# A one-core hybrid encoder block: the second half of an expert's down product moves behind the load of the next expert's class

## The reference

```python
def expert_block(args):
    xb, e = args
    return (jax.nn.silu(xb @ w_gate[e]) * (xb @ w_up[e])) @ w_down[e]
...
y = y_pad[dest] * gate_s[:, None].astype(y_pad.dtype)
out = jnp.zeros((T, D), y.dtype).at[tok_s].add(y)
```

## Time and profile before

| | us |
|---|---|
| median of 3 runs | 1718.0 |
| lowest, highest run | 1713.45, 1719.99 |
| the profiled execution: its own time | 1719.35 |
| the profiled execution: span from first to last instruction | 1717.5 |
| PE busy in that span | 1667.0 (97%) |
| DVE, ACT, POOL busy | 746.9, 476.6, 526.0 |

### The profile page before, as it was taken

The page is one execution under the profiler, slowest core; times in us unless marked ns, Lnnn a source line. Parts: engine busy times, 40 slices in busy tenths (PEclk is TensorE's granted clock), DMA queues, the critical chain, the costliest instruction groups (busy, mean ns, idle before and its releaser), DMA issues.

```text
span 1717.5 us, 30945 instructions
## 1 busy us (share of the span) xinstructions
PE 1667.0 (97%) x10740; PEld 1220.9 (71%) x10741; DVE 746.9 (43%) x1756; ACT 476.6 (28%) x1258; POOL 526.0 (31%) x617
## 2 busy tenths in 40 slices
PE   8899999999999999999998899999999999999996
PEld 6667676676756667576657688688778787878784
DVE  1444556544555445555466323332333333333323
ACT  1444333433233342443333111111111111111111
POOL 0101011010110101011012446556565555655553
PEclk9999999999999999999999999999999999999998
DMA  9732233323433234322234879989999999999995
GB/s 345 187 113 69 88 125 116 100 72 98 127 116 92 72 105 128 116 81 79 86 122 151 298 270 366 331 302 344 336 352 360 317 332 326 358 328 355 332 326 168
DMA packets 180051, 360.23 MB, mean 210 GB/s; under 512 B 34806, under 2 KB 65883, under 8 KB 180005
## 3 DMA queue, kind: packets, MB, share of 16 engines
q1 hardware_dynamic: 152980, 304.25, 53.1%
q0 software_dynamic: 26160, 55.26, 9.2%
q10 hardware_dynamic: 864, 0.10, 0.0%
HBM read 311.52 MB, written 76.68 MB: 226 GB/s over the span
## 4 chain that ended last, share of the span: by engine, by line
PE 77%; issue 8%; DMA 5%; DVE 3%; SPq 3%; POOL 2%; ACT 1%; DVEq 0%; ACTq 0%; POOLq 0%
PE bank L366 14%; PE bank L358 13%; PE bank L389 13%; PE bank L1515 10%; PE bank L1502 10%; PE bank L1520 8%; DMA h_dram<-sums_quarters,movec 2%; DMA sums_quarters<-h_dram,movec 2%; PE bank L408 1%; PE bank L521 1%; PE bank L424 1%; SPq L223 1%; POOL xg L1422 1%; PE bank L502 1%; ACT L1566 1%
## 5 line engine op out<-in xcount | busy, mean ns | idle before, releaser
L1502 PEld LDWEIGHTS bank<-xT,wts 128*128 128x128 f32 x2048 | 253.8, 194 | 34.1 <-issue 28.0
L366 PE MATMUL bank<-uT,w_in_sb 128*128 128x128 f32 x2304 | 274.2, 277 | 0.6 <-DMA w_in_sb<-w_in_in 0.6
L366 PEld LDWEIGHTS bank<-uT,w_in_sb 128*128 128x128 f32 x2304 | 263.6, 192 | 12.7 <-issue 10.4
L1502 PE MATMUL bank<-xT,wts 128*128 128x128 f32 (+2 forms) x2048 | 259.2, 287 | 13.8 <-issue 6.0
L358 PE MATMUL bank<-w_in_sb,uT 128*128 128x512 f32 (+1 forms) x768 | 262.3, 494 | 4.9 <-DVE attm L858 2.8
L1515 PE MATMUL bank<-xT,wts 128*128 128x128 f32 (+2 forms) x2048 | 249.8, 283 | 1.9 <-DVE hT L1619 1.9
L1515 PEld LDWEIGHTS bank<-xT,wts 128*128 128x128 f32 x2048 | 246.7, 192 | 2.1 <-DVE hT L1619 2.1
L1034 POOL TENSOR_SCALAR ss<-ss 128x1 f32<-128x1 f32 (+1 forms) x48 | 9.7, 202 | 741.9 <-ACT junk L605 405.5
L1520 PE MATMUL bank<-wts,hT 128*128 128x512 f32 x512 | 232.2, 597 | 0.0
L389 PE MATMUL bank<-w_out_sb,mixT 128*128 128x512 f32 x512 | 223.2, 593 | 0.8 <-ACT mixT L631 0.8
L1422 POOL DMA_INDIRECT xg<-v_dram,idxm x165 | 195.4, 1185 | 67.8 <-issue 32.0
(11 more groups left out here) (263 smaller groups left out, 1737.8 us busy)
## 6 DMA issues: line engine op xcount, KB each, us to landing
wts<-w_gate_in SPq DMA_DIRECT2D x32, 2048.0 KB
wts<-w_up_in SPq DMA_DIRECT2D x32, 2048.0 KB
wts<-w_down_in SPq DMA_DIRECT2D x32, 2048.0 KB
p_dram<-decays_keys_gates SPq DMA_DIRECT2D x60, 192.0 KB, 3.2
pT<-p_dram SPq DMA_DIRECT2D x15, 768.0 KB, 4.3
x_sb<-x_in SPq DMA_DIRECT2D x16, 512.0 KB, 3.5
xT_in<-x_t_in SPq DMA_DIRECT2D x16, 512.0 KB, 4.8
h_sb<-x_in SPq DMA_DIRECT2D x16, 512.0 KB, 5.1
```

The costliest lines, as they stand in the source:

```text
L366: m = pe.matmul(bk[name][0:hi - lo, col:col + P], w_in[:, k, lo:hi], uT[:, k, :], start=k == 0, stop=k == KD - 1)
L1502: m = pe.matmul(G[m_ % 2][:, 0:w], wg[:, k, m_ * P:(m_ + 1) * P], xT[:, k, 0:w], start=k == 0, stop=k == KD - 1)
```

## The change

The second half of the down product leaves `pe_chunk` and becomes `pe_second`, which is one piece of code for all classes. TensorE's loop is rotated: the first half of expert 0 stands ahead of the loop (in all three classes), then for each following expert the class is loaded, the second half of the expert before is done, and then the branch on the class leads to gate, up and first half of this expert. The quarter means' product now stands amid the second half, and for every expert, narrow ones too.

```diff
@@ -1538,12 +1538,15 @@
         pe_down(pe, YB[0], n, 0, main, range(KF - 1, KF)).then_inc(sem("m_d_done"), 2 if w == P else 1)
-        if w > P:
-            after(pe, "m_", "tail_square", n + 1)
-            pe.wait_ge(sem("fw_loaded"), 6 * 16)
-            pe.matmul(U[0][:, 0:2], quad[:, :], part[:, :], start=True, stop=True)
+
+    def pe_second(pe, n):
+
         after(pe, "m_", "summed", 3 * n)
-        pe_down(pe, YB[1], n, 1, main, range(KF)).then_inc(sem("m_d_done"), 1)
+        pe_down(pe, YB[1], n, 1, slice(0, P), range(2))
+        after(pe, "m_", "tail_square", n + 1)
+        pe.wait_ge(sem("fw_loaded"), 6 * 16)
+        pe.matmul(U[0][:, 0:2], quad[:, :], part[:, :], start=True, stop=True)
+        pe_down(pe, YB[1], n, 1, slice(0, P), range(2, KF)).then_inc(sem("m_d_done"), 1)
@@ -1857,8 +1860,12 @@
             pe.wait_ge(sem("meta_ready"), 1)
-            with pe.Fori(0, NE) as e:
-                by_width(pe, chunk_class(pe, e), lambda w: pe_chunk(pe, e, w))
+            by_width(pe, chunk_class(pe, 0), lambda w: pe_chunk(pe, 0, w))
+            with pe.Fori(1, NE) as e:
+                cls = chunk_class(pe, e)
+                pe_second(pe, e - 1)
+                by_width(pe, cls, lambda w: pe_chunk(pe, e, w))
+            pe_second(pe, NE - 1)
```

More of the change, by code:

```diff
@@ L1659, in dve_y_over @@
             .then_inc(sem("o_yD_taken"), 1)
-    return (credit, load, first_base, move, put_sums, scatter_over, gather, gather_over, copy_pieces, copy_index, pe_x_over, pe_chunk, pe_chunk_over, act_silu, act_gate,
+    return (credit, load, first_base, move, put_sums, scatter_over, gather, gather_over, copy_pieces, copy_index, pe_x_over, pe_chunk, pe_second, pe_chunk_over, act_silu, act_gate,
             act_squares, act_rows_over, dve_x, dve_x_over, dve_h, dve_tail, dve_sums, dve_scale, dve_clear, dve_y_over)
@@ L1774, in program @@
         with ExitStack() as mem:
-            (credit, load, first_base, move, put_sums, scatter_over, gather, gather_over, copy_pieces, copy_index, pe_x_over, pe_chunk, pe_chunk_over, act_silu, act_gate,
+            (credit, load, first_base, move, put_sums, scatter_over, gather, gather_over, copy_pieces, copy_index, pe_x_over, pe_chunk, pe_second, pe_chunk_over, act_silu, act_gate,
              act_squares, act_rows_over, dve_x, dve_x_over, dve_h, dve_tail, dve_sums, dve_scale, dve_clear,
```

## The result

| | before | changed |
|---|---|---|
| median of 3 runs, us | 1718.0 | 1748.19 |
| lowest, highest | 1713.45, 1719.99 | 1743.77, 1749.08 |
| ratio, 95% interval | | 1.018 (1.0154 to 1.0207) |
| profiled execution: span, us | 1717.5 | 1741.7 |
| profiled execution: own time, us | 1719.35 | 1743.77 |

The change makes the kernel slower by 1.8%, 30 us of the medians and 24.2 us of the two profiled spans. The point forecast was 1738, the range 1726 to 1749; one of the three executions, at 1749.08, lies just above that range.

A forecast was written before the change was run, and what follows sets the result against it. The expert loop was taken as bound by what PE is given, transfers close behind; wide experts -5.9, narrow experts +18 and code fetches +7.5 us on 1718 gave 1738, range 1726 to 1749.

The forecast's parts named there:

- The three terms: Expert loop: wide experts -5.9 us, narrow experts' new wait +18, code fetches at first visits after the rotation +7.5.
- The signs that the prediction named: Squares' waits of 18 to 25 us at narrow experts, none at wide; PE idle about 5 us between halves at experts 0, 1.
- Wide experts, forecast -5.9 us: At 14 wide experts the squares' wait goes: 0.36 us each, 0.8 more from six; bound -10.4.
- Narrow experts, forecast +18: 18 narrow experts get the product and its wait; 15 lose 1.34 us on average; bounds 10 and 22.
- its count of 20.1: Sum over 15 narrow experts of the later gate load, before 2 us off for longer rounds.
- Rival B: Narrow experts' squares come in time, leaving 0.22 us each, 3.3 us: +4.9 in all, 1723; chance 0.10.
- the slot: Quarter means' product's place at narrow experts, behind twelve passes, 4.84 us after the down product's start.
- The rotation's code, forecast +7.5: First visits fetch code: +3.0 at expert 0, about 5.3 at expert 1, -0.8 at expert 2; bounds 0 and +13.
- bound of 13: Upper bound of the code term, if code is fetched again later or the loop's end adds one more.
- the 0.4 us and the -0.8 us: Sequencer's shorter path to expert 0's gate, 0.4 us; more cover for the branch into expert 2's class, -0.8.
- The clock "in full from expert 3 on": Expected sign: PE's clock stays granted in full, 2.4 GHz, from expert 3 on in the changed kernel.
- Rival D: Transfers, at 0.95 to 0.99 of their time, become the bound: a few microseconds either way; no chance of its own.

The follow-up runs named there:

- experiment 1: Loop rotated as in the change, quarter means' product kept in the wide classes' code ahead of the second half; against the kernel before: 1741.36 us, ratio 1.0147.
- experiment 3: Kernel before, not rotated, with the quarter means' product amid the second half for wide experts only: 1709.03 us, ratio 0.9957.
- experiment 10: Kernel before, not rotated, wide experts only, with the quarter means' product behind one product of the second half: 1706.28 us, ratio 0.9961.
- experiment 2: Kernel before, not rotated, with the quarter means' product amid the second half for all experts: 1741.28 us, ratio 1.0135.
- experiment 4: Changed kernel with the quarter means' product behind three of the second half's products instead of two: 1735.63 us, ratio 1.0113 to the kernel before.
- experiment 8: Changed kernel with the quarter means' product behind all four products of the second half: 1733.57 us, ratio 1.0092 to the kernel before.
- experiment 9: Kernel before, not rotated, with the quarter means' product ahead of the second half for all experts: 1773.23 us, ratio 1.037.
- experiment 6: Kernel before with only a copy of expert 0's code ahead of the loop, nothing rotated: 1719.74 us, ratio 1.0029.
- experiment 5: Changed kernel run once more, unedited: 1744.22 us, ratio 1.0157 to the kernel before.
- experiment 7: Changed kernel with a copy of the narrow class alone ahead of the loop: 1737.15 us, ratio 1.013 to the kernel before.

## Why the prediction was right, and where its sizes were off

**Direction and mechanism.** Right. The three terms are there: the wait for the squares at narrow experts, the one gained at wide ones, and fetches of code in the first rounds. The signs that the prediction named held: 24.2 us of waits at the narrow experts and none at the wide ones, and idle times of 3.87 and 4.95 us between the halves of experts 0 and 1. What the rotation was to hide, the load of the class, was hidden already; experiment 1 shows that the rotation by itself can even bring it out.

**Wide experts, forecast -5.9 us.** Measured -5.5 in the profiled execution, 0.36 at each expert without a longer wait, as worked out, and -7.3 and -5.8 by the medians of experiments 3 and 10, which hold this part alone. Shown.

**Narrow experts, forecast +18.** Measured +15.0. The 1.66 us from squares to gate load is right; the prediction took 2 us off its count of 20.1, and 5 would have been right. The squares come 6.08 us after the down product's first load on average from expert 9 on, against 6.39 in the kernel before, but that is not a general gain of the longer rounds: it is all in experts 12 and 19, where the squares came at 7.18 and 8.94 us before and at 6.08 and 6.37 in the changed kernel. The other eleven have 6.08 before and 6.05 after. With expert 4 (6.73 and 5.62) these three account for 4.8 of the 5 us. At expert 19 VectorE had waited 2.30 us for the rows that it adds to (`sums_quarters`) in the kernel before; whether the longer rounds or chance took that away is not shown. Experiments 2, 4, 8 and 9 move only the place, and the loss moves with it: ahead 61 us of the whole, part of it by the lower clock, behind two 25 (not rotated); and in the rotated kernels the steady part falls from 9.2 us over the one before to 0.2 behind three. Rival B fails by this: the earliest squares come at 5.55 us, and the slot, as the prediction worked it out, is at 4.84.

**The rotation's code, forecast +7.5.** This is the term that was mis-sized: 14.7 us, above even the bound of 13 that I gave it. By rounds, from gate product to gate product and with the wide experts' gain set apart, experts 0, 1 and 2 give +1.5, +3.5 and -2.4, together 2.7 us where the forecast counted 7.5. About 3.6 us of that shortfall come from the execution of the kernel before, whose expert 0 was slow; without it they would give 6.3, by estimate. Experts 5, 6 and 7 give +3.3, +1.7 and +5.4, together 10.4 us, and the point forecast had nothing there, only its bound: this is the step that was missing. So the term is not the rotation's alone. In experiment 1, the rotation without the wait in the shared half, 2.5 us are left for it.

At expert 5 the kernel before idled 1.69 us on the way into the 160 class. Where narrow experts do not wait for the squares it is 1.7 to 2.9 us (the kernel before, experiments 1, 3, 6 and 10), and where they wait amid or behind the second half it is 3.1 to 5.0 us (the changed kernel and experiments 2, 4, 5, 7 and 8), whether the loop is rotated or not. That fits a sequencer that comes to the branch only when the wait is over and then has four passes or fewer to hide the fetch. No run singles it out; experiment 9, with eight passes behind the wait, has no idle time there. At expert 7 the branch out of the middle class idles PE for 5.65 us.

The clock is the other part that was left out. The prediction priced each fetch as idle time, but behind this idle time the passes run at 1.2 GHz for a while: 0.50 in the windows behind the idle time of experts 0, 5 and 7, 0.58 behind that of expert 1. The kernel before had this as well, at expert 1, where expert 2's gate and up product took 19.72 us instead of the 17.35 of the changed kernel; that is the -2.4 above. What the change adds is the lower clock behind experts 0, 5 and 7: expert 6's gate and up product takes 19.03 us instead of 17.35. No run shows by themselves the 0.4 us and the -0.8 us that the forecast put on the sequencer's shorter path and on the better cover of expert 2.

**The clock "in full from expert 3 on"** was wrong: it fell again at experts 5 and 7. So was the reading of the earlier trace rows from which it came. A 9 there is a mean of 90% or more over 43 us, and the clock of the kernel before was at its lower level behind expert 1's idle time, as the window shows. PE's own row has an 8 in the slices from 902 to 988 us, the second of which lies wholly in the expert loop. Rival D did not show; DMA share is 0.94 and 0.96 in the two windows.

**The sum.** With the measured terms -5.5 + 15.0 + 14.7 = 24.2, the span's difference. The profiled execution is the fastest of the changed kernel's three runs, so the median is another 4.4 us over that. The errors ran against each other, 3 us too much at the narrow experts and 7 too little for the code, and the median lies 10 us above the point forecast and less than 1 us inside the range. The direction was foreseen; that the number stayed inside was partly luck.

**What stays open.** Why the branch at expert 7 needs a fetch in the changed kernel and in experiments 4, 5 and 8, less of one in 7, and none in 1. All of the first four have the full copy and the product in the shared half; experiment 2, with the product amid the second half but no rotation, has no such idle time at expert 7 either. That the cuts between the 16 KB lines fall otherwise would explain it; this was only argued, since the line in which an instruction lies is in no view. Open too is why a few executions lose far less: 1729.55 us for the changed kernel in experiment 5, 1715.16 and 1719.41 in experiment 8. Their mean granted clock is higher (0.993 against 0.987 to 0.989 in the other executions of experiment 5, 0.994 and 0.991 against 0.986 to 0.990 in those of experiment 8), so the lower clock is part of it; whether fetches are too, no trace tells.

## What to carry to other kernels

The load of the class and the branches cost nothing here while eight passes were queued; before moving such a load, look at the interval between the last product ahead of it and the first behind it. A wait that is merged into code shared by all classes is paid by the classes that never needed it: moving the product amid the second half for the wide class alone gains 0.4%, for all it loses 1.4%. And where a sequencer can be held by a wait, count the instructions between that wait and the next piece of work: in experiments 1 and 2 they came on top of it. A profile's row of slices hides a lower clock that lasts a few microseconds; windows around each idle time show it.

## What the runs showed of the hardware

- Idle times that I read as fetches of code: 3.87, 4.95, 3.12 and 5.65 us of PE in the changed kernel, and 9.32 us with two packets on the instruction queue (experiment 6). All are in the first eight rounds of the loop, and from 1156 to 1650 us no trace has a packet on that queue.
- Behind a wait of 2.20 us in the middle of float32 products the granted clock fell from 2.4 to 1.2 GHz for part of the next eight passes, 5.38 us instead of 3.68; behind one of 2.10 us at the next narrow expert it did not, and it did behind one of 1.76 and not behind one of 2.22 us (experiment 9). PE's idle times of up to 1.31 us at narrow experts of the changed kernel left the clock at 1.00 in the windows from 1300 to 1500 us.
- The sequencer seems to stop at a product whose semaphore is not there yet: branch, back edge and load of a register behind it add 1.04 us to the path (experiment 1), and four queued passes behind the wait, 1.6 us, fall 0.2 to 0.6 us short of back edge, load and branch (experiment 2).
